# State space layer: the second part's C products behind the first part's states on VectorE, latent keys and values copied ahead of the last high halves

## The reference, cut to what matters

```python
in_re = f_re * bu_re - f_im * bu_im            # B products of u, per group of 16 channels, 64 states
in_im = f_re * bu_im + f_im * bu_re
_, _, s_re, s_im = lax.associative_scan(_complex_linear_combine, (a_re_t, a_im_t, in_re, in_im), axis=1)
y = (jnp.einsum('blgp,gcp->blgc', s_re, c_re) - jnp.einsum('blgp,gcp->blgc', s_im, c_im))
y = jax.nn.gelu(y.reshape(bsz, seq, SSM_WIDTH) + d_skip * uf)
```

```python
kv = (rms_norm_2(c_kv, kv_norm) @ w_ukv).reshape(B, S, MLA_HEADS, MLA_NOPE + MLA_V)
k_nope, v = kv[..., :MLA_NOPE], kv[..., MLA_NOPE:]
```

## Time and profile before

| | us |
|---|---|
| Median of three runs (lowest, highest) | 1267.54 (1267.04, 1268.5) |
| The profiled execution, its own time | 1267.45 |
| Its span, from the first instruction to the last | 1265.6 |
| TensorE busy | 1233.7 (97%) |
| VectorE busy | 907.4 (72%) |
| ScalarE busy | 643.0 (51%) |
| GpSimd busy | 104.2 (8%) |
| Mean clock granted to TensorE | 0.997 of full |

### The profile page before, as it was taken

The page is one execution under the profiler, slowest core; times in us unless marked ns, Lnnn a source line. Parts: engine busy times, 40 slices in busy tenths (PEclk is TensorE's granted clock), DMA queues, the critical chain, the costliest instruction groups (busy, mean ns, idle before and its releaser), DMA issues.

```text
span 1265.6 us, 19059 instructions
## 1 busy us (share of the span) xinstructions
PE 1233.7 (97%) x7605; PEld 1037.8 (82%) x7605; DVE 907.4 (72%) x1463; ACT 643.0 (51%) x1042; POOL 104.2 (8%) x163
## 2 busy tenths in 40 slices
PE   7999999999999999999999999999999999999998
PEld 3566778888988888887999987978888787999986
DVE  7998877666688998687555645588997686665553
ACT  4344555775547664545443543556665545444341
POOL 6400011101000200201000002000200201000000
PEclk9999999999999999999999999999999999999999
DMA  7636575435565546355666665464545355655552
GB/s 261 207 94 197 166 227 188 138 120 164 159 179 165 150 150 192 124 166 168 211 186 184 183 189 158 164 201 158 157 150 182 127 168 167 198 184 184 184 189 76
DMA packets 71959, 215.76 MB, mean 170 GB/s; under 512 B 16256, under 2 KB 19744, under 8 KB 71744
## 3 DMA queue, kind: packets, MB, share of 16 engines
q1 hardware_dynamic: 65008, 206.43, 51.6%
q0 software_dynamic: 2112, 6.97, 1.8%
q10 hardware_dynamic: 4752, 1.14, 0.4%
HBM read 209.01 MB, written 3.15 MB: 168 GB/s over the span
## 4 chain that ended last, share of the span: by engine, by line
PE 83%; DVE 8%; ACT 5%; issue 2%; DMA 1%; POOL 1%; SPq 0%; DVEq 0%; POOLq 0%; ACTq 0%
PE acc L692 17%; PE acc L694 17%; PE acc L693 17%; PE acc L671 7%; PE acc L670 7%; PE acc L672 7%; PE acc L631 3%; DVE weights_lo L1769 1%; PE mixed L1006 1%; ACT junk L1273 1%; PE mixed L1107 1%; ACT weights_hi L1239 1%; DMA weights_raw<-stream_dram 1%; PE turned L1061 1%; DVE h_T L1799 1%
## 5 line engine op out<-in xcount | busy, mean ns | idle before, releaser
L1769 DVE TENSOR_TENSOR weights_lo<-weights_raw,weights_hi 128x1024 fp32r<-128x1024 f32 (+1 forms) x304 | 356.1, 1206 | 72.1 <-ACT weights_hi L1239 71.2
L1239 ACT ACTIVATE weights_hi<-weights_raw 128x1024 fp32r<-128x1024 f32 (+1 forms) x304 | 304.6, 1042 | 76.2 <-DMA weights_raw<-stream_dram 75.9
L692 PE MATMUL acc<-weights_hi,act_F_hi 128*128 128x512 f32 (+1 forms) x680 | 276.4, 406 | 7.0 <-DVE act_F_lo L1799 2.9
L694 PE MATMUL acc<-weights_hi,act_F_lo 128*128 128x512 f32 (+1 forms) x680 | 267.5, 393 | 0.0
L693 PE MATMUL acc<-weights_lo,act_F_hi 128*128 128x512 f32 (+1 forms) x680 | 267.3, 393 | 0.0
L670 PE MATMUL acc<-act_F_hi,weights_hi 128*128 128x256 f32 x624 | 177.3, 284 | 0.0
L672 PE MATMUL acc<-act_F_lo,weights_hi 128*128 128x256 f32 x624 | 176.1, 282 | 0.0
L671 PE MATMUL acc<-act_F_hi,weights_lo 128*128 128x256 f32 x624 | 175.9, 282 | 0.0
L692 PEld LDWEIGHTS acc<-weights_hi,act_F_hi 128*128 128x128 f32 x680 | 128.3, 189 | 38.6 <-issue 4.6
L694 PEld LDWEIGHTS acc<-weights_hi,act_F_lo 128*128 128x128 f32 x680 | 128.0, 188 | 28.9
L693 PEld LDWEIGHTS acc<-weights_lo,act_F_hi 128*128 128x128 f32 x680 | 128.5, 189 | 26.5
(11 more groups left out here) (336 smaller groups left out, 1964.3 us busy)
## 6 DMA issues: line engine op xcount, KB each, us to landing
weights_raw<-stream_dram SPq DMA_DIRECT2D x306, 512.0 KB, 3.6
weights_raw_more<-stream_dram SPq DMA_DIRECT2D x58, 512.0 KB, 3.7
gains<-rows_dram POOLq DMA_DIRECT2D x12, 512.0 KB, 4.6
weights_raw<-stream_dram SPq DMA_DIRECT2D x6, 416.0 KB, 3.2
weights_raw<-stream_dram SPq DMA_DIRECT2D x4, 384.0 KB, 3.3
x_T<-x_in_dram SPq DMA_DIRECT2D x4, 256.0 KB, 6.7
ssm_bc<-ssm_bc_dram SPq DMA_DIRECT2D x1, 1024.0 KB, 9.1
u_scratch<-u_T ACTq DMA_DIRECT2D x4, 256.0 KB, 3.8
```

The lines of the kernel that those rows point to most:

```text
L692: pe.matmul(o, xh, wh, start=first and kk == 0, stop=False)
L694: i = pe.matmul(o, xl, wh, start=False, stop=last and kk == s["nk"] - 1)
L1239: act.activation(high(s, slice(0, n)), whole(s, slice(0, n)), ACT.Copy).then_inc(hi_made, 1)
L1769: dve.tensor_tensor(low(s, slice(0, n)), whole(s, slice(0, n)), high(s, slice(0, n)).bitcast(F32), ALU.subtract).then_inc(lo_made, 1)
```

## The change

Two edits. On VectorE the call that makes part 1's C products moves from behind `c_mats(0)` to behind `scan_states(0)`. On ScalarE `run` makes the high halves up to two slots less before it takes out a `ukv` chunk, so that two high halves stand behind the copies of latent keys and values where they stood ahead. Nothing is added or removed; TensorE, SP and GpSimd have the same orders as before.

```diff
@@ ScalarE, run()
                 for name, end in chunks_ending(pos, pos + n):
-                    splits(end + AHEAD)
+
+                    splits(end + AHEAD - (2 if ".ukv." in name else 0))
                     evac(name)
@@ VectorE, the state space layer
             b_mats(0)
             c_mats(0)
-            c_mats(1)
             b_mats(1)
             turns_from(NSUB // 4, (ev[:, 0, :], ev[:, 1, :]), 1)
             turns_from(NSUB // 2, (par[:, 16, :], par[:, 17, :]), 2)
             scan_states(0)
+            c_mats(1)
             b_mats(2)
```

## The result

The changed kernel took 1271.64 us (median of 9 runs, 1269.36 to 1271.97) against 1267.6 for the kernel before (9 runs, 1267.04 to 1268.5): a ratio of 1.0026 (1.0018 to 1.0035, over all runs; the two medians alone stand 0.32% apart), slower by 0.26%. Forecast were 1270.9 us, a range of 1269.0 to 1273.0, and 0.70 for slower by over 0.2%. The profiled execution took 1270.84, its span is 1269.0; that is 3.39 more than the 1267.45 of before, where the sum said 3.4. The median is 4.0 above.

A forecast was written before the change was run, and what follows sets the result against it. TensorE bounds the kernel over most of the span, VectorE from 39.6 to 78.4 us. Delay 4.46 plus clock 1.0 minus latent copies 2.1 gave +3.4 us on 1267.45, forecast 1270.9, range 1269.0 to 1273.0.

The forecast's parts named there:

- the sum: Whole kernel: 4.46 + 1.0 - 2.1 = +3.4 us on the profiled execution's 1267.45.
- three signs of being wrong: Wait before part 1's states below 1 us; delay at 101 us gone at 150; `mla_v_T` still among TensorE's waits.
- The gap costs and brings nothing: VectorE ahead of 39.6 us: removing 5.35 us of products buys no earlier start, leaving about 5.5 us idle.
- +4.67 for the products, -0.21 for part 1's B products: VectorE, 39.6 to 78.4 us: moved products cost 4.67, faster B products give 0.21; part 1's scan ends 4.46 later.
- The waits: TensorE, new waits: 2.0 us before `taps(2)` at 69.11, and 3.2 us for part 1's states.
- The clock term, +1.0: TensorE behind its wait for part 1's states: a fall to half clock costs 1.0 us, between 0 and 1.5.
- edit 1's 5.46: State space layer: 4.46 us of delay to part 1's scan plus 1.0 us for the clock.
- The upper bound of 1.5: Part 1's states products at half clock throughout: 3.53 - 2.03 = 1.5 us.
- The rival without a fall on the path: TensorE at part 1's states: no clock fall on the path, then +2.4 us, 1269.9; chance 0.32.
- Edit 2, -2.1: Start of `ret.0`, both layers: waits for latent copies go, 1.24 + 1.14, less a new 0.2 wait; 2.1 us taken.
- The rival in which edit 2 gives nothing: At `ret.0`, the wait on the values becomes one on lower halves; then +5.5 us, 1273.0; chance 0.10.
- The rival in which the delay is taken up: VectorE has slack between 59.5 and 78.4 us, edit 1 costs nothing; only edit 2's -2.1 remains, 1265.4; chance 0.03.

The follow-up runs named there:

- the filled gap: Changed kernel plus four unread products on VectorE where part 1's C products had stood; 1271.05 us, ratio 1.0029.
- the second profile of the changed kernel: Trace from the unaltered changed kernel, measured again beside the last experiments against the kernel before; 1271.2 us, ratio 1.0027.
- edit 1 alone: Kernel before with only part 1's C products moved behind part 0's states, ScalarE's order as before; 1273.2 us, ratio 1.0046.
- the kernel with the late products: Changed kernel with part 1's C products directly ahead of `scan_states(1)` instead of behind `scan_states(0)`; 1271.32 us, ratio 1.0037.
- filling the waits: Changed kernel plus seven unread TensorE matmuls: two before `states_part(0)`, two before `taps(2)`, three before `states_part(1)`; 1271.38 us, ratio 1.0032.
- the doubled products: Changed kernel plus four unread products on VectorE behind `scan_states(0)`, ahead of part 1's C products; 1276.77 us, ratio 1.0074.
- Moving part 2's products: Kernel with edit 2 and early transposes, with part 2's C products moved from ahead of part 1's scan to behind it; 1265.38 us, ratio 0.9986.
- edit 2 alone: Kernel before with only ScalarE's edit, two high halves behind the latent copies; VectorE's order as before; 1266.29 us, ratio 0.9989.
- early transposes: Kernel with edit 2 only, TensorE making part 0's taps and transposes one weight slot earlier; 1264.62 us, ratio 0.9978.
- early transposes with moved products: Changed kernel, both edits, with TensorE making part 0's taps and transposes one weight slot earlier; 1268.2 us, ratio 1.0001.
- the three kernels with spare matmuls: Unread TensorE matmuls placed in waits: changed kernel plus sixteen, 1275.48 us; plus seven, 1271.38; late-products kernel (products directly before `scan_states(1)`) plus seven, 1272.07.

## Why the prediction held, step by step

The time came out as forecast, and not all of the mechanism did. The prediction named three signs of being wrong, and one of them came: the wait before part 1's states stayed below 1 us (0.29). The other two did not: the delay at 101 us is there at 150 (5.22 and 5.24), and `mla_v_T` is gone from TensorE's waits.

**The gap costs and brings nothing.** Confirmed by the 8.24 us of VectorE's bracket, by the start of part 1's B products, 39.75 against 39.60, and by the filled gap. The size was off: 5.5 us were forecast. VectorE was done with part 0's C products at 31.5 and not at 34.0, mostly because they started at 26.55 and not at 28.52 in this execution, and in part because these four took 4.95 us and not 5.55. The early start is of the execution and not of the change: in the second profile of the changed kernel they started at 28.75 and the idle time was 6.94, with edit 1 alone 28.10 and 5.94. Idle time that ends with another engine's work costs nothing, so the sum didn't feel it.

**+4.67 for the products, -0.21 for part 1's B products.** Both as measured: 59.44 to 64.11, and 39.75 to 46.89, 7.14 us instead of 7.36. The states were written at 83.05; forecast 82.9. The 0.21 rested on GpSimd being done earlier. Its small operations took 0.23 to 0.29 us each while VectorE idled:

```profile
33.63 0.29 POOL L2609 TENSOR_TENSOR turn_step<-turn_step 128x64 f32<-128x64 f32 x1
33.88 0.25 POOL L2609 TENSOR_TENSOR ssm_par<-turn_step 128x32 f32<-128x32 f32 x1
```

In the kernel before the same two stood beside the C products and took 1.15 and 1.23. The Trainium skill (SBUF — State Buffer, Who interferes with whom) says that a VectorE instruction with two inputs in SBUF contends with a GpSimd instruction that reads SBUF, for a pair of ports that one of them holds at a time. These two rows agree, and so do the C products' 4.67 us instead of 5.35.

**The waits.** Before `taps(2)`: forecast 2.0, measured 2.07. Before part 1's states: forecast 3.2, measured 0.29. This is the step that failed in its mechanism. I had written that a fall of the clock behind the first wait would cost nothing, since it would eat into the second, and then priced one behind the second. In the trace it was the first that came. It lasted from 70.7 to 77.5 us, over most of the work between the two waits, and ate 2.9 of the 3.2 us. Behind the short second wait no other fall came.

**The clock term, +1.0.** The profiled execution has no such cost behind the states. It has 0.62 us more of an idle piece that the forecast didn't have (1.02 instead of 0.40), and TensorE's start at part 1's states is 4.61 late, 0.15 above the 4.46 of the sum. 4.61 + 0.62 = 5.23, the shift of 5.22 at 84 us. So of edit 1's 5.46 in the forecast 4.46 was right in size and cause, and the 1.0 was replaced by 0.77 from elsewhere: it came out right for a wrong reason. That a half clock behind a wait on the path costs something like it, 1.2 us, the kernel with the late products showed. The upper bound of 1.5 was taken from the wrong row: it compares part 0's products with part 2's unbroken 2.03 us, while part 1's own row in the kernel before, its idle piece included, took 2.79. How much of the changed kernel's median is clock stays open: filling the waits kept the clock up and won 1.4 us up to 84 us, but an idle piece and a new wait of 0.21 us took it back. The rival without a fall on the path described the profiled execution better in its mechanism, but its 1269.9 lacks the idle piece. The rule of the Trainium skill (TensorE: Matmul & The Clock Gate, Part 1), that idling brings the half clock back, agrees in its direction with the waits of 2.07 and 5.42 us and with the fall not coming behind 0.29. A wait of 2.09 that left the clock alone stands in the last section.

**Edit 2, -2.1.** Measured 0.92 + 1.19 = 2.1 at the two places in the trace and 1.9 between 344 and 1200 us, as the shift drifts up by 0.2 elsewhere; 1.3 and 1.6 by the medians, within the bounds of 1.0 and 2.4. The wait for `mla_v_T` is gone and the wait for the third slot's lower half in the first layer is there: TensorE lost 0.4 us at it (a shift of 3.99 to 4.37 from 351.8 us on) where 0.2 was said. The rival in which edit 2 gives nothing is out.

**No place takes the delay back.** The shift is 5.22 at 84 us, 5.21 at 113, 5.28 at 344. The rival in which the delay is taken up falls, and the doubled products (+5.1 us for 4.67) say the same. Moving part 2's products gained nothing either.

**The sum.** Forecast +3.4, the profiled execution +3.4, the medians +4.0 and +3.4.

## What to carry to other kernels

Work may be free where it stands, if its engine would wait there anyway; moving it away from such a place gains nothing, and moving it into a stretch without a gap costs all of it. So before moving work off a path, find the wait that ends the stretch ahead of it and ask what ends that wait: here TensorE's transposes, and putting these one slot of weights earlier gained 1.7 us by the medians without touching VectorE. When two waits of an engine follow each other, a slower clock behind the first shortens the second: price the pair, not each.

## What the runs showed of the hardware

**An idle piece that belongs to a place in the instruction stream.** In part 1's states products (128 matmuls of 64x128) TensorE stood still ahead of the last seven, with no releaser. Its length goes with the wait just before the 128. Wait and piece in us: before 0.83 and 0.40, edit 2 alone 0.71 and 0.75, changed 0.29 and 1.02, edit 1 alone 0 and 1.51, doubled 0 and 1.58, part 2's products moved 0 and 1.25; with a wait of 1.55 (gap filled), 2.33 (early transposes) or 5.42 (late products) there was none. The sum is 1.2 to 1.6 wherever there is a piece in this row (the changed kernel's second profile: 0 and 1.18, early transposes with moved products: 0 and 1.50). In the three kernels with spare matmuls this row has no piece, not even with a wait of 0 or 0.46 us before it, and one stands in part 2's states products. There its place goes by the count of TensorE's instructions: with 14 more ahead (seven spare matmuls, two instructions each; pieces of 0.81 and 0.80) it is ahead of the last 7, and with 32 more (sixteen of them), 18 earlier in the same row, in both cases behind 1104 matmul instructions of TensorE. Without spare matmuls it is behind 724. Why it goes from the one count to the other is open:

```profile
107.47 1.73 PE L900 MATMUL turned<-c_mats_alt,states 64*32 64x128 f32 x103
109.59 0.64 PE L900 MATMUL turned<-c_mats_alt,states 64*32 64x128 f32 x25 [0.40 <-issue]
```

A guess that would fit the waits: something of some 1.5 us has to come to TensorE at certain points of its instructions and can do so while it waits for another engine. What it is, no run here shows.

**A fall of the clock that lasts.** At the wait that ends at 59.6 the clock was at half for 3 to 4 us, at the one that ends at 71.3 for 6.8 (edit 1 alone: about 10), though TensorE worked on without a gap behind it. The same wait left it at 1.00 in the kernel with edit 1 alone, where the 128 matmuls behind it took 2.03 us:

```profile
59.46 2.03 PE L900 MATMUL turned<-c_mats_alt,states 64*32 64x128 f32 x128 [2.09 <-DVE states L1803]
```

So a wait of two microseconds may or may not bring the fall, and a forecast can give it no more than a chance. Nor is a short wait safe: the changed kernel's falls from 787 and 1074 us came behind two waits each, of 0.70 and 0.75 and of 0.75 and 0.75 us, two microseconds apart.
